# First expert's rows: gathered and transposed in one product, with x as the weights

## The chip, the core and the metric

The kernel runs on one core of a Trainium2 chip. The metric is the device time of one execution in microseconds. Inside the core, TensorE (PE in the profile) multiplies, VectorE (DVE), ScalarE (ACT) and GpSimd (POOL) work on vectors, and SyncE (SP) issues nearly all the DMA transfers. Each of them runs its own list of instructions in order and waits on semaphores for the others.

## The reference

A decoder block on 256 tokens of width 1024, in f32: three groups of attention heads, a memory attention, and then a layer of routed experts. Only the last is touched here:

```
logits = h @ w_router + b_router                  # h = rmsnorm(x), 256 x 1024
gate   = softmax over the 4 largest of 32 logits  # each token picks 4 of 32 experts
for each expert e:
    hh  = h @ w_e1[e] + b_e1[e]                   # 1024 -> 2048, even columns glu, odd columns lin
    act = min(glu, 7) * sigmoid(1.702 glu) * (clip(lin) + 1) * gate
    y  += act @ w_e2[e] + gate * b_e2[e]          # 1024 -> 1024
```

## The kernel before

The expert layer keeps 256 rows of x times a gain in `H` (128 partitions, two row blocks t of 1024 columns). An expert takes at most 64 of the rows in one step (`SLOTS`). The rows are picked by a product with a one-hot matrix: `hot` is 128x64 for each of the two row blocks, with the reciprocal root of the norm in place of the ones. `gather` (L642) uses `hot[:, t, :]` as the weights (64 columns) and 512 columns of `H` as the moving side; the two column halves h go to partitions 0 to 63 and 64 to 127 of one PSUM bank (`B_GATHER`), each half summed over t. That is 4 products. `xg_leaves` (ACT, L1290) copies the bank to `xg`, `turn_gathered` (PE, L653) turns it in 4 transposes, because `multiply_w1` (L693) needs the model dimension on the partitions, and `xgT_leaves` (ACT, L1297) copies the result to `xgT`.

The weights of the experts stream through a ring of 10 slots of 2 MB (`ring`). An expert uses 6 of them: 4 for `w_e1` (two blocks c each), 2 for `w_e2`. SP refills a slot when PE has given it back: the last product of a slot increments `w1_used` (L710) or `w2_used` (L730), for which `load_group` (L889) waits. The 10 slots are filled once before the expert layer begins; slot 0 is the first to be refilled, after the first two blocks c of expert 0 (`multiply_w1(0, ..., 0)` and `(0, ..., 1)`).

For every expert but the first, `gather` and `turn_gathered` stand between blocks of the expert before (L777, L779, L788, L790, and in `step`, L749), where PE has other work. For expert 0 there is none. There the order on PE is (L771 to L776): `gather(0)`, `keep_busy(2)` (two products of the identity with itself, whose result nobody reads), `turn_gathered(0)`, `turn_gates` (L635: two transposes of the gates, which the scatter's biases need), and then the eight `multiply_w1(0, ...)`. DVE makes the first one-hot matrix at L1768 and signals `hot_made`. POOL makes those of the following experts (L1025), into the same tile `hot`, once `gathered` says that the last one has been read. On ACT the order is `xg_leaves(0)`, `xgT_leaves(0)`, `gates_leave` (L1328 to L1330).

A product of f32 operands appears in the trace as two records, a transpose as one.

Of the kernel before, what the change touches and what calls it, by code (L numbers as in the profile page):

```python
# [14 lines left out]
P = 128  # L15
D = 1024
T = 256
NT = T // P
KC = D // P
# [11 lines left out]
SLOTS = 64  # L31
# [28 lines left out]
B_W1, B_W2, B_SCAT, B_GATHER, B_HID = 0, 2, 3, 5, 6  # L60


def build(nc, x, mem, positions, g_mix, w_in, b_forget, g_qa, g_ka, g_cq, g_ckv, w_uq, w_ukv,
# [4 lines left out]
    def at(name, shape, off, dt=F32):  # L68
        return nc.alloc_sbuf_tensor_at(name, shape, dt, offset=base + off)
# [42 lines left out]
    H = at("h_sb", [P, NT, D], Z + 8192)  # L112
    OT = at("heads_T", [P, KC, T], Z + 8192)
    b1T = at("b1_T", [P, E, 16], Z + 16384)
    hot = at("hot_slot", [P, NT, SLOTS], Z + 18432)
# [44 lines left out]
    PS = nc.alloc_psum_tensor("banks", [P, 8, 512], F32)  # L160
# [3 lines left out]
    def S(name):  # L164

        if name not in sems:
            sems[name] = nc.alloc_semaphore(name)
        return sems[name]

    V, G, A, TE = nc.vector, nc.gpsimd, nc.scalar, nc.tensor  # L170
# [67 lines left out]
    def row_cols(q):  # L238

        a = P * W1_ROWS * (q // W1_ROWS) + q % W1_ROWS  # L240
        return slice(a, a + W1_ROWS * (P - 1) + 1, W1_ROWS)

    def hidden_cols(q, par):

        a = 2 * (P * W2_ROWS * (q // W2_ROWS) + q % W2_ROWS) + par
        return slice(a, a + 2 * W2_ROWS * (P - 1) + 1, 2 * W2_ROWS)
# [24 lines left out]
    def _(pe):  # L271
# [26 lines left out]
        def keep_busy(n):  # L298

            pe.wait_ge(S("turned_out"), turn.n - 3)  # L300
            for _ in range(n):
                TE.matmul(PS[:, turn.n % 4, 0:P], ident[:], ident[:], start=True, stop=True)
# [13 lines left out]
        def rows(t):  # L316
            return lambda c: hT[:, c, t * P:(t + 1) * P]
# [62 lines left out]
        for t in range(NT):  # L380
# [4 lines left out]
            for c in range(KC):  # L385
                if (t, c) == (0, KC // 2):
                    pe.wait_ge(S("w_in_cq_rest_in"), 16)
                ins = TE.matmul(bank[:, 0:Q_RANK], rows(t)(c), win["cq"][:, c, :], start=(c == 0), stop=(c == KC - 1))
# [33 lines left out]
        for h in range(FOX_H):  # L422
# [4 lines left out]
                      stop=True).then_inc(S("mm_done"), 1)  # L427
# [71 lines left out]
        for k in range(8):  # L499
            ins = TE.transpose(bank[:, 64 * k:64 * k + 64], b1s[:, hidden_cols(k // 2, k % 2)], ident[0:64, 0:64])  # L500
# [134 lines left out]
        def turn_gates():  # L635

            pe.wait_ge(S("gates_doubled"), 1)
            for t in range(NT):
                ins = TE.transpose(PS[0:3 * E, B_HID, P * t:P * t + P], gate_twice[:, t, :], ident[:])
            ins.then_inc(S("gates_turned"), 1)  # L640

        def gather(i):  # L642

            pe.wait_ge(S("hot_made"), i + 1)
            if not (isinstance(i, int) and i == 0):
                pe.wait_ge(S("xgT_out"), i)
            for t in range(NT):
                for h in range(2):
                    ins = TE.matmul(PS[SLOTS * h:SLOTS * h + SLOTS, B_GATHER, :], hot[:, t, :],  # L649
                                    H[:, t, 512 * h:512 * h + 512], start=(t == 0), stop=(t == NT - 1))  # L650
            ins.then_inc(S("gathered"), 1)

        def turn_gathered(i):  # L653

            pe.wait_ge(S("xg_out"), i + 1)
            for q in range(KC // 2):
                ins = TE.transpose(PS[:, B_GATHER, P * q:P * q + P], xg[:, row_cols(q)], ident[:])  # L657
            ins.then_inc(S("xg_turned"), 1)
# [90 lines left out]
        def step(g, q):  # L749

            i = GROUP * g + (2 + q)
            w1, w2 = of_group(g, PER_STEP * q), of_group(g, PER_STEP * q + W1_UNITS)
            for c in range(KC):
                multiply_w1(i, w1, c)
                if c == AT_TURN:
                    turn_hot(i - 2)
                if c in AT_SCATTER:
                    scatter(i - 2, AT_SCATTER.index(c))
                if c == AT_GATHER:
                    gather(i + 1)  # L760
                if c == AT_GATHER_TURN:
                    turn_gathered(i + 1)
            for k in range(KC // 2):
                multiply_w2(i - 1, w2, k)
                if k == AT_HIDDEN:
                    turn_hidden(i)

        pe.wait_ge(S("turned_out"), turn.n)
        pe.wait_ge(S("mm_out"), len(left_no))
        pe.wait_ge(S("rows_gained"), NT)  # L770
        gather(0)  # L771
        keep_busy(2)
        turn_gathered(0)
        turn_gates()
        for c in range(KC):
            multiply_w1(0, first(0), c)  # L776
            if c == AT_GATHER:  # L777
                gather(1)
            if c == AT_GATHER_TURN:  # L779
                turn_gathered(1)  # L780
# [279 lines left out]
    def _(act):  # L1060
# [212 lines left out]
        for half in range(2):  # L1273
            act.wait_ge(S("mm_out"), left_no[f"mo1{half}"])
            ins = A.activation(junk_x2[:, 512 * half:512 * half + 512], X[:, 1, 512 * half:512 * half + 512], ACT.Square,
                               accum_out=x2_half[:, half:half + 1])
# [4 lines left out]
        for t in range(NT):  # L1281
            ins = A.activation(rt[:, 4, t, 0:E], rt[:, 0, t, 0:E], ACT.Exp, bias=rt[:, 2, t, 0:1])
        ins.then_inc(S("gates_exped"), 1)

        def gates_leave():

            act.wait_ge(S("gates_turned"), 1)
            A.copy(rt_gateT[0:3 * E, :], PS[0:3 * E, B_HID, 0:T]).then_inc(S("gateT_out"), 1)

        def xg_leaves(i):  # L1290

            act.wait_ge(S("gathered"), i + 1)
            if not (isinstance(i, int) and i == 0):
                act.wait_ge(S("xg_turned"), i)
            A.copy(xg[:], PS[:, B_GATHER, :]).then_inc(S("xg_out"), 1)  # L1295

        def xgT_leaves(i):  # L1297

            act.wait_ge(S("xg_turned"), i + 1)
            if not (isinstance(i, int) and i == 0):  # L1300
                act.wait_ge(S("w1_used"), W1_UNITS * i)
            A.copy(xgT[:].rearrange("p q h s -> p (q h s)"), PS[:, B_GATHER, :]).then_inc(S("xgT_out"), 1)
# [22 lines left out]
            act.wait_ge(S("hot_turned"), i + 1)  # L1325
            A.copy(hotT[:], PS[:, B_SCAT, 0:T]).then_inc(S("hotT_out"), 1)  # L1326

        xg_leaves(0)  # L1328
        xgT_leaves(0)
        gates_leave()  # L1330
        xg_leaves(1)
        hidden_leaves(0)
# [549 lines left out]
```

## Time and profile before

| | |
|---|---|
| median of 3 runs | 1132.28 us (1130.17 to 1132.37) |
| the profiled execution, its own time | 1132.49 us |
| its span, first to last instruction | 1130.8 us |
| mean granted TensorE clock | 0.998 |
| PE busy | 1085.5 us (96%), 5069 instructions |
| DVE, ACT, POOL busy | 318.2, 192.1, 138.9 us |
| read from HBM | 427.67 MB, 379 GB/s over the span |

The profiled execution took 0.21 us more than the median of the runs, and 1.7 us of its time lie outside the span. PE's busy time is a modelled one, since its products are pipelined; two products that lie side by side in the array count for themselves.

### The profile page before, as it was taken

How to read it: one execution, taken by the hardware profiler on the slowest of the kernel's cores; microseconds unless marked ns; L12 is line 12 of the kernel's file. 1: busy time of each engine (PE TensorE's matmuls, PEld its weight loads, DVE VectorE, ACT ScalarE, POOL GpSimd, SP SyncE). 2: the span in 40 equal slices, each digit the busy share in tenths (PEclk: the TensorE clock that was granted, in tenths of full speed). 3: DMA queues.
4: the chain of work that ended last, by engine and by line, in shares of the span. 5: the costliest groups of instructions: out<-in, count | busy, mean ns of one | idle time of the engine just before them, and what ended most of it. 6: DMA issues, size and time to landing. Idle time of an engine off the chain costs nothing.

```text
span 1130.8 us, 13638 instructions
## 1 busy us (share of the span) xinstructions
PE 1085.5 (96%) x5069; PEld 439.3 (39%) x5069; DVE 318.2 (28%) x664; ACT 192.1 (17%) x389; POOL 138.9 (12%) x291
## 2 busy tenths in 40 slices
PE   6999999999999999999999999999999999999997
PEld 4566856533333333333333333333333333333332
DVE  4477754412222222222222222222121111222222
ACT  1144433211111111111111111111101111110111
POOL 1032300211111111111111111011111111111100
PEclk9999999999999999999999999999999999999999
DMA  6913376499999999999999999999999999999995
GB/s 225 365 38 150 126 296 281 183 431 426 428 428 427 427 428 429 429 428 428 428 430 429 428 428 429 429 428 429 427 429 429 428 428 428 429 429 428 428 428 235
DMA packets 44024, 429.06 MB, mean 379 GB/s; under 512 B 6336, under 2 KB 13792, under 8 KB 19168
## 3 DMA queue, kind: packets, MB, share of 16 engines
q1 hardware_dynamic: 43376, 427.67, 90.3%
q10 hardware_dynamic: 624, 1.07, 0.2%
q8 instruction: 15, 0.25, 0.1%
q14 instruction: 9, 0.07, 0.0%
HBM read 427.67 MB, written 1.05 MB: 379 GB/s over the span
## 4 chain that ended last, share of the span: by engine, by line
PE 64%; DMA 29%; DVE 3%; SPq 1%; ACT 1%; issue 1%; DVEq 0%
DMA ring<-in_w_e_dram 27%; PE banks L706 27%; PE banks L726 13%; PE banks L313 8%; PE banks L649 4%; PE banks L676 4%; PE banks L739 2%; PE banks L657 2%; DMA w_in_qk<-in_w_in_dram 1%; SPq L830 1%; PE banks L295 1%; PE banks L528 1%; PE banks L330 1%; PE banks L665 1%; PE banks L346 0%
## 5 line engine op out<-in xcount | busy, mean ns | idle before, releaser
L706 PE MATMUL banks<-ring,xg_T 128*64 128x512 f32 x2048 | 478.3, 599 | 24.6 <-DMA ring<-in_w_e_dram 23.5
L706 PEld LDWEIGHTS banks<-ring,xg_T 128*64 128x64 f32 x2048 | 135.8, 136 | 306.3 <-issue 254.3
L726 PE MATMUL banks<-ring,act_T 128*64 128x512 f32 x1024 | 232.9, 596 | 0.4 <-DVE act_T L1828 0.4
L1800 DVE TENSOR_TENSOR x_sb<-x_sb,banks 128x1024 f32<-128x1024 f32 x64 | 78.2, 1221 | 414.9 <-PE banks L676 382.8
L726 PEld LDWEIGHTS banks<-ring,act_T 128*64 128x64 f32 x1024 | 70.3, 137 | 132.5 <-issue 128.1
L1810 DVE TENSOR_TENSOR glu<-banks,b_T 128x512 f32<-128x512 f32 x32 | 22.1, 692 | 242.1 <-PE banks L739 242.1
L1039 POOL COPY picked<-slot_table 128x2 f32 (+1 forms) x32 | 6.0, 188 | 563.2 <-PE banks L665 563.2
L676 PE MATMUL banks<-y_sb,hot_gate_T 64*128 64x512 f32 x256 | 72.0, 640 | 0.8 <-ACT y_sb L1322 0.8
L1309 ACT COPY hidden<-banks 128x1024 f32<-128x1024 f32 x32 | 32.4, 1012 | 206.6 <-PE banks L706 206.6
L1295 ACT COPY xg_rows<-banks 128x512 f32<-128x512 f32 x33 | 19.3, 585 | 271.7 <-PE banks L649 271.7
L649 PE MATMUL banks<-h_sb,hot_slot 128*64 128x512 f32 x264 | 63.0, 598 | 0.9 <-DVE hot_slot L1768 0.9
L1322 ACT COPY y_sb<-banks 128x512 f32<-128x512 f32 x32 | 18.7, 585 | 202.0 <-PE banks L726 202.0
L1043 POOL TENSOR_SCALAR hot_gate<-iota,picked 128x128 f32<-128x128 f32 x64 | 50.1, 791 | 5.5 <-issue 5.5
L739 PEld LDWEIGHTS banks<-ident,hidden 128*128 128x128 f32 x256 | 31.0, 194 | 26.0 <-issue 26.0
L676 PEld LDWEIGHTS banks<-y_sb,hot_gate_T 64*128 64x128 f32 x256 | 19.4, 184 | 52.3 <-issue 51.5
L1828 DVE TENSOR_TENSOR act_T<-lin,sig 128x512 f32<-128x512 f32 x32 | 22.2, 693 | 60.3 <-ACT sig L1316 59.4
L739 PE MATMUL banks<-ident,hidden 128*128 128x128 f32 x256 | 37.1, 288 | 0.0
L1031 POOL TENSOR_SCALAR hot_slot<-iota,picked,stat 128x64 f32<-128x64 f32 x64 | 36.2, 577 | 5.5 <-issue 5.5
L1028 POOL COPY picked<-slot_table 128x2 f32 (+1 forms) x32 | 6.0, 186 | 230.7 <-PE banks L649 230.7
L649 PEld LDWEIGHTS banks<-h_sb,hot_slot 128*64 128x64 f32 x264 | 19.1, 137 | 37.9 <-issue 37.9
L1326 ACT COPY hot_gate_T<-banks 128x256 f32<-128x256 f32 x32 | 11.9, 372 | 100.7 <-PE banks L665 100.7
L313 PE MATMUL banks<-w_out_sb,heads_T 128*128 128x512 f32 x64 | 29.0, 598 | 0.0
(304 smaller groups left out, 774.0 us busy)
## 6 DMA issues: line engine op xcount, KB each, us to landing
ring<-in_w_e_dram SPq DMA_DIRECT2D x190, 2048.0 KB, 37.9
w_out_sb<-in_w_out_dram SPq DMA_DIRECT2D x1, 4096.0 KB, 13.8
ring<-in_w_e_dram SPq DMA_DIRECT2D x4, 1024.0 KB, 40.8
w_in_qk<-in_w_in_dram SPq DMA_DIRECT2D x1, 2048.0 KB, 15.1
w_mkv_sb<-in_w_mkv_dram SPq DMA_DIRECT2D x1, 2048.0 KB, 10.7
w_in_cq<-in_w_in_dram SPq DMA_DIRECT2D x2, 768.0 KB, 8.2
w_in_qc<-in_w_in_dram SPq DMA_DIRECT2D x1, 1536.0 KB, 17.0
w_in_kc<-in_w_in_dram SPq DMA_DIRECT2D x1, 1536.0 KB, 15.1
```

The costliest lines, as they stand in the source:

```text
L313: ins = TE.matmul(bank[:, 0:r.shape[-1]], l, r, start=(c == 0), stop=(c == n - 1))
L649: ins = TE.matmul(PS[SLOTS * h:SLOTS * h + SLOTS, B_GATHER, :], hot[:, t, :], H[:, t, 512 * h:512 * h + 512], start=(t == 0), stop=(t == N ...
L657: ins = TE.transpose(PS[:, B_GATHER, P * q:P * q + P], xg[:, row_cols(q)], ident[:])
L676: ins = TE.matmul(PS[:, first + h, :], hotT[a:a + SLOTS, t * P:(t + 1) * P], Ys[a:a + SLOTS, :], start=True, stop=True)
L706: ins = TE.matmul(PS[SLOTS * h:SLOTS * h + SLOTS, B_W1 + b, :], left, ring[slot][:, 2 * F * j + F * h + 512 * b:2 * F * j + F * h + 512 * ...
L726: ins = TE.matmul(PS[SLOTS * h:SLOTS * h + SLOTS, B_W2, :], actT[:, c % 4, c // 4, :], ring[slot][:, D * j + 512 * h:D * j + 512 * h + 512 ...
L739: ins = TE.transpose(PS[:, B_HID + par, P * q:P * q + P], Hs[:, hidden_cols(q, par)], ident[:])
L1031: ins = G.tensor_scalar(hot[:, t, :], iota[:, 0:SLOTS], pick[:, 0, t:t + 1], y2[t], ALU.is_equal, ALU.mult)
L1043: ins = G.tensor_scalar(hotg[:, t, :], iota[:], pick[:, 1, t:t + 1], pick[:, 2, t:t + 1], ALU.is_equal, ALU.mult)
L1309: A.copy(Hs[:], PS[:, B_W1:B_W1 + 2, :].rearrange("p b n -> p (b n)")).then_inc(S("hidden_out"), 1)
L1800: V.tensor_tensor(X[:, t, :], X[:, t, :], PS[:, first:first + 2, :].rearrange("p b n -> p (b n)"), ALU.add).then_inc(S("added"), 1)
L1828: V.tensor_tensor(actT[:], lin[:], sig[:], ALU.mult).then_inc(S("act_ready"), 1)
```

## The change

For expert 0 alone, gather and transposition become one product with the sides swapped: 128 columns of `H` (every second one, the order that `multiply_w1` wants) are the weights, and `hot[:, t, :]`, 64 columns wide, is the moving side. The result is the transposed rows, and it stands in `B_GATHER` as the four transposes would have left it. `gather(0)`, `keep_busy(2)`, `turn_gathered(0)` and the first `xg_leaves` go. The count `gathered`, for which POOL and ACT wait, is now raised by the first of the two gate transposes, and `xg_out` by a bare semaphore increment on ACT.

```
         def turn_gates():
             pe.wait_ge(S("gates_doubled"), 1)
             for t in range(NT):
                 ins = TE.transpose(PS[0:3 * E, B_HID, P * t:P * t + P], gate_twice[:, t, :], ident[:])
-            ins.then_inc(S("gates_turned"), 1)
+                ins.then_inc(S("gathered" if t == 0 else "gates_turned"), 1)

+        def gather_turned():
+            pe.wait_ge(S("hot_made"), 1)
+            for q in range(KC // 2):
+                for h in range(2):
+                    cols = row_cols(q)
+                    cols = slice(512 * h + cols.start, 512 * h + cols.stop, cols.step)
+                    for t in range(NT):
+                        ins = TE.matmul(PS[:, B_GATHER, P * q + SLOTS * h:P * q + SLOTS * h + SLOTS], H[:, t, cols],
+                                        hot[:, t, :], start=(t == 0), stop=(t == NT - 1))
+            ins.then_inc(S("xg_turned"), 1)

         pe.wait_ge(S("rows_gained"), NT)
-        gather(0)
-        keep_busy(2)
-        turn_gathered(0)
+        gather_turned()
         turn_gates()
         for c in range(KC):
             multiply_w1(0, first(0), c)

-        xg_leaves(0)
         xgT_leaves(0)
+        act.sem_inc(S("xg_out"), 1)
         gates_leave()
```

## Rows read from the trace of the kernel before

**Rows 1.** Page, part 2: 40 slices of the span, PE and DMA busy.
```profile
PE   6999999999999999999999999999999999999997
...
DMA  6913376499999999999999999999999999999995
```
**Rows 2.** Stretches: length, PE busy (records), granted clock, DMA share, GB/s.
```profile
222.50:223.00 0.50, 0.50 (x4) 1.00 0.00 0
...
223.00:223.50 0.50, 0.50 (x4) 1.00 1.07 229
...
230.00:690.00 460.00, 459.41 (x2122) 1.00 1.01 428
...
690.00:1090.00 400.00, 376.71 (x1720) 1.00 1.01 429
...
1114.00:1131.00 17.00, 10.97 (x48) 0.95 0.27 106
```
**Rows 3.** SP's issues of ring slots: start us, us, engine line, transfer, count.
```profile
222.45 3.76 SPq L844 DMA_DIRECT2D ring<-in_w_e_dram  x2
...
231.03 0.33 SPq L844 DMA_DIRECT2D ring<-in_w_e_dram  x1
...
235.30 0.33 SPq L844 DMA_DIRECT2D ring<-in_w_e_dram  x1
...
240.59 5.01 SPq L847 DMA_DIRECT2D ring<-in_w_e_dram  x2
```
**Rows 4.** Timeline, the path from the one-hot matrix to expert 0.
```profile
212.70 0.54 DVE L1768 TENSOR_SCALAR hot_slot<-iota,slot_table,stat 128x64 f32<-128x64 f32 x2
...
213.39 2.60 PE L649 MATMUL banks<-h_sb,hot_slot 128*64 128x512 f32 x8 [0.88 <-DVE hot_slot L1768]
...
215.92 1.22 PE L302 MATMUL banks<-ident 128*128 128x128 f32 x4
...
216.03 0.58 ACT L1295 COPY xg_rows<-banks 128x512 f32<-128x512 f32 x1 [2.15 <-PE banks L649]
...
216.94 1.06 PE L657 MATMUL banks<-ident,xg_rows 128*128 128x128 f32 x4
...
217.79 0.46 PE L639 MATMUL banks<-ident,gate_twice 128*96 128x128 f32 x2
...
218.03 0.58 ACT L1302 COPY xg_T<-banks 128x512 f32<-128x512 f32 x1 [1.42 <-PE banks L657]
...
218.76 8.81 PE L706 MATMUL banks<-ring,xg_T 128*64 128x512 f32 x40 [0.52 <-ACT xg_T L1302]
```
**Rows 5.** Stretches of 0.5 us around it, as in Rows 2.
```profile
212.50:213.00 0.50, 0.01 (x1) 1.00 0.99 426
...
214.00:214.50 0.50, 0.50 (x6) 1.00 0.84 360
...
214.50:215.00 0.50, 0.50 (x4) 0.52 1.07 459
...
217.00:217.50 0.50, 0.50 (x4) 0.50 0.00 0
...
217.50:218.00 0.50, 0.50 (x5) 0.57 0.00 0
```
**Rows 6.** Timeline, gather and transposes of later experts, at full clock.
```profile
246.78 1.89 PE L649 MATMUL banks<-h_sb,hot_slot 128*64 128x512 f32 x8
...
248.72 0.58 ACT L1295 COPY xg_rows<-banks 128x512 f32<-128x512 f32 x1 [4.74 <-PE banks L649]
...
252.03 0.74 PE L657 MATMUL banks<-ident,xg_rows 128*128 128x128 f32 x4
```
**Rows 7.** Timeline, keep_busy's products at full clock.
```profile
209.00 1.28 PE L302 MATMUL banks<-ident 128*128 128x128 f32 x10
```
**Rows 8.** Timeline, products with 128 weight columns and few moving columns; PEld loads weights.
```profile
211.87 0.30 PEld L632 LDWEIGHTS banks<-route,upper 128*128 128x128 f32 x2
...
164.82 1.31 PEld L358 LDWEIGHTS banks<-upper,head_squares 128*128 128x128 f32 x11 [0.24 <-issue]
```
**Rows 9.** Timeline, what stands by the path: DVE's gates, POOL's next matrix, its reader.
```profile
215.00 0.18 DVE L1781 COPY gate_twice<-route 128x64 f32<-128x64 f32 x1
...
216.16 0.18 POOL L1028 COPY picked<-slot_table 128x2 f32<-128x2 f32 x1 [8.28 <-PE banks L649]
...
216.55 1.15 POOL L1031 TENSOR_SCALAR hot_slot<-iota,picked,stat 128x64 f32<-128x64 f32 x2 [0.20 <-issue]
...
227.37 1.92 PE L649 MATMUL banks<-h_sb,hot_slot 128*64 128x512 f32 x8
```

## The prediction

> **What bounds the kernel now.** I read the page's slices first. PE and the DMA engines both show nines from slice 8 on [rows 1]; before that the DMA engines are often idle. Two full rows don't say which of the two sets the end, so the table of stretches comes next: from 230 to 690 us PE is busy for 459.41 of 460 us and the DMA share is 1.01; from 690 to 1090 us PE has 376.71 of 400 us, and the DMA share is still 1.01 [rows 2]. PE is the faster of the two: it lives off the filled ring at first and is starved from 690 us on. The DMA stream is never interrupted. A slot of 2.097 MB at 428 GB/s takes 4.9 us; the 192 slots of the 32 experts less the 10 filled ahead leave 182, and 182 x 4.9 = 892 us. From the moment at which the stream starts, 223.1 us [rows 2], that reaches 1115 us, and from there on the DMA share is low [rows 2]. So the end of the kernel is the start of the stream plus a fixed length plus a fixed tail of PE work. What a change before the expert loop is worth is how much earlier or later SP issues the first refill, at 222.45 us [rows 3].
>
> That refill waits for PE to finish the first two blocks of expert 0. These begin at 218.76 us, when ACT has copied xg_T; in front of this stands a chain in which every engine waits for the one before: the one-hot matrix ready at 213.24, gather 213.39, copy 216.03, transposes 216.94, copy 218.03, expert 0 at 218.76 [rows 4]. It is 5.37 us from 213.39 to 218.76, with nothing beside it. The change rewrites just this chain.
>
> The last thing to read there is the clock. It is full up to 214.5 us, then half (0.50, 1.2 GHz) and full again from about 217.8 us; before the fall PE had little to do (0.01 us of work between 212.5 and 213.0) [rows 5]. The old chain ran mostly at half rate: the gather's 8 records took 2.60 us and the 4 transposes 1.06 us, against 1.89 and 0.74 us at full rate [rows 4, 6].
>
> **Part by part: what goes.** At the full clock the old chain would take 1.89 + 0.05 to the copy [rows 6], 0.58 for the copy, about 0.14 to the transposes, 0.74 + 0.05, 0.58 for the second copy and 0.15 to the first product (218.03 + 0.58 to 218.76 [rows 4]): 4.2 us. All this but the last 0.78 us goes: 3.4 us at full rate, 4.6 us as profiled (213.39 to 218.03). keep_busy's four records (1.22 us [rows 4]) lie beside the first copy, so their removal saves at most the 0.1 us by which they may delay the transposes.
>
> **What comes.** 4 q x 2 h x 2 t = 16 products, 32 records, each with a load of 128 weight columns and a stream of 64 columns. No row shows this shape. The stream alone would be short: 128 columns cost (1.28 - 0.28) / 9 = 0.11 us a record [rows 7], so 64 cost 0.055. The loads decide: with one moving column, 11 loads take 1.31 us, (1.31 - 0.19) / 10 = 0.11 us apart, and with 32 moving columns two are 0.11 apart too (0.30 - 0.19) [rows 8]. The bounds are 0.055 and 0.11 us a record; I take 0.11, since the rows with fewer moving columns than 64 all stand there. The stride of two columns in the weights is new for a load of this kind; the transposes, whose data have that stride too, take 1.06 us for 4 at half rate [rows 4] and 0.74 at full rate [rows 6] and give no sign of more than 0.11 a load. At full rate: 31 x 0.11 + 0.27 for the last = 3.7 us. At half rate a record takes (1.22 - 0.58) / 3 = 0.21 us (keep_busy's, between 215.92 and 217.14 [rows 4]).
>
> The Trainium skill (TensorEngine Tiling (Array Packing), section When to Use Tiling) speaks against this change: where the right-hand side is 64 columns or fewer it advises to swap the sides and to use two column tiles, which is the old form. The same skill (TensorE: Matmul & The Clock Gate, section LDWEIGHTS) has a load last as long as its columns divided by 1.2, 107 ns here, whatever streams; by it the new product is 32 x 0.107 = 3.4 us, an estimate from that page, and [rows 8] agree.
>
> **The sum.** PE's idle time before 213.39 us is untouched, so the clock's fall at 214.5 stays. Until then 1.1 us run at full rate: 10 records. Half rate to 217.8: 3.3 / 0.21 = 15 records. The last 7 at full rate: 0.8 us. The product ends at 213.39 + 1.1 + 3.3 + 0.8 + 0.2 (the last one's tail) = 218.8 us. Then 0.04 + 0.58 for ACT's copy and 0.15: expert 0 begins at 219.5 to 219.6, where it was 218.76. That is 0.8 us later. Never slowed, it would be 213.39 + 3.7 + 0.8 = 217.9, against 213.39 + 4.2 = 217.6 for the old chain, 0.3 us later. The new form trades one copy and its two hand-overs for twice as many weight loads as the old chain had, 32 against 12, each twice as wide as the gather's.
>
> Costed at nothing: turn_gates, 0.46 us [rows 4], now runs beside ACT's copy of 0.58 us, and the gates are ready at 215.18 [rows 9]. POOL's next one-hot matrix waits for `gathered`, now raised behind the whole product, at about 219 instead of 216.1; it needs 0.18 + 0.2 + 1.15 us [rows 9] and is read at 227.37, so 6 us of cover remain; behind it on POOL stand only the following matrices. On ACT the increment costs no copy, and xg_leaves(1) waits for the second gather anyway. The refills behind the first: the stream needs the second at 228, third at 232.9, fourth at 237.8 us, and SP issued them at 225.9, 231.03 and 235.30 [rows 3]; with 0.6 us from issue to the first packet there are 1.2 us and more of slack, and they move together with the first. So a delay at the start goes to the end once, neither more nor less: profiled 1132.49 + 0.8 = 1133.3 us, and against the median 1132.28 + 0.8 = 1133.1 us.
>
> **The rivals** follow.
>
> **Half rate lasts longer (slower).** The new product keeps the array's columns streaming for only half of each record's time, then PE stands for 0.7 us before expert 0 and nothing like keep_busy fills that gap. If the clock does not return at 217.8 us, the product ends 1.1 us later for its last 7 records and tail, and the 16 records before the first refill, 0.215 us each at full rate (1.89 / 8 less the tail [rows 6]), take up to 0.43: together 0.8 + 0.8 = 1.6 us if the clock returns as expert 0 begins, 5 us if only after the first refill. I take the middle, 3.3 us: 1135.6 us. It decides against me if the clock stays at 0.50 beyond about 220 us. For it speaks the half-empty array; against it, that the clock came back in the old chain in spite of its gaps.
>
> **The half rate does not come (faster).** If PE keeps its clock in this chain, expert 0 begins at 217.9, 0.9 us before the profiled one: 1131.4 us. The fall came 1.1 us into the gather, and the runs of before lie 2.2 us apart, about what such a stretch costs, so it may not come every time.
>
> **The stream sets the product (faster).** If loads hide behind one another, 32 x 0.055 = 1.8 us at full rate, about 2.4 with the half-rate part: expert 0 at 216.6, 2.1 us gained: 1130.2 us. [rows 8] speak against it.
>
> **The change does nothing:** were the start of the stream not on the path, the time would stay at 1132.3. [rows 2] speak against it, but a time can't tell it from my forecast.
>
> **How the numbers follow.** Forecast, 0.3 to 1.6 us later: 0.57. Longer half rate: 0.19. No half rate: 0.14. Stream-set: 0.05. Nothing: 0.05. 0.2% is 2.26 us, about what a measurement of this kernel can tell from no change: below 1130.0 or above 1134.5 us. Faster by that takes the stream-set case and a bit of luck: 0.06. Slower takes most of the longer half rate and little else: 0.18. The same: 0.76. The range goes from the stream-set case, 1130.2, to a little beyond the middle of the longer half rate, 1136.2.
>
> **What would show it.** In the profile after: 32 records of the new line, 0.11 us apart at full rate and 0.21 at half, between 213.4 and about 218.8 us; ACT's copy right behind; gate transposes inside that copy; the first record of expert 0 at 219.5 (right if 218.9 to 220.3); half rate over before 218 us; the first refill at 223.2 in place of 222.45, and all later refills and the end later by the same. I am wrong if records stand 0.06 us apart, if the clock stays at 0.50 beyond 220 us, or if the end moves by something other than the first refill.

## The result

| | kernel before | changed kernel |
|---|---|---|
| median | 1131.74 us (10 runs, 1130.17 to 1135.08) | 1135.94 us (10 runs, 1134.05 to 1138.33) |
| ratio | 1 | 1.0029 (95% interval 1.0018 to 1.004) |
| profiled execution, time and span | 1132.49, 1130.8 us | 1134.16, 1132.4 us |
| granted clock of the executions (mean over each) | 0.998 in the profiled one | 0.994 to 0.996 |

The changed kernel is slower by 0.3%. In a second comparison it was 1138.06 us (5 runs) against 1132.29 (29 runs), ratio 1.0045 (1.0032 to 1.0058); the two intervals overlap. The profiled execution of the changed kernel is one of its mildest (1134.16 us of 1134.05 to 1138.33), so the profile shows less than the whole loss.

The page's slices are as before but for PE's first digit and a dip of the clock in the eighth slice, 198 to 226 us (PE, its clock, DMA):

```profile
PE   7999999999999999999999999999999999999997
...
PEclk9999999899999999999999999999999999999999
...
DMA  6913376499999999999999999999999999999995
```

The chain of the changed kernel, from its timeline (start us, us, engine line, records), answers to [rows 4]:

```profile
213.16 5.34 PE L661 MATMUL banks<-hot_slot,h_sb 128*128 128x64 f32 x32 [0.88 <-DVE hot_slot L1778]
...
218.29 0.63 PE L639 MATMUL banks<-ident,gate_twice 128*96 128x128 f32 x2
218.54 0.58 ACT L1312 COPY xg_T<-banks 128x512 f32<-128x512 f32 x1 [4.88 <-PE banks L661]
...
219.27 10.20 PE L718 MATMUL banks<-ring,xg_T 128*64 128x512 f32 x40 [0.34 <-ACT xg_T L1312]
```

From the start of the new product to the first product of expert 0 it takes 6.11 us; the old chain took 5.37 us. The copy follows at once and the gate transposes lie beside it. But that is 0.74 us of a difference that grows: SP issues the first refill at 224.34 us, 11.18 us after the chain began, where it was 9.06 (222.45 less 213.39 [rows 3, 4]). The refills behind it follow as before:

```profile
224.34 0.33 SPq L854 DMA_DIRECT2D ring<-in_w_e_dram  x1
227.78 0.33 SPq L854 DMA_DIRECT2D ring<-in_w_e_dram  x1
232.93 0.33 SPq L854 DMA_DIRECT2D ring<-in_w_e_dram  x1
237.20 0.33 SPq L854 DMA_DIRECT2D ring<-in_w_e_dram  x1
```

The table of stretches (length, PE busy and records, granted clock, DMA share, GB/s) says where the other 1.38 us (11.18 less 9.06 less 0.74) come from:

```profile
215.00:215.50 0.50, 0.50 (x5) 0.79 0.99 426
215.50:222.00 6.50, 6.16 (x25) 0.50 0.09 37
222.00:222.50 0.50, 0.50 (x6) 0.89 0.00 0
...
230.00:690.00 460.00, 459.41 (x2122) 1.00 1.01 428
690.00:1090.00 400.00, 376.94 (x1720) 1.00 1.01 428
```

Half rate begins at about 215.3 us, 2.1 us into the new product, and lasts until about 222.1 us, 2.8 us into the products of expert 0. Before the change it lasted from 214.5 to about 217.9 us [rows 5]: 6.8 us against 3.4. The last two lines match [rows 2] within 0.3 us of PE's busy time: nothing happens to the expert loop itself.

### The profile page after: what moved, and what is told of

Read it like the earlier page. It is cut to its first block, busy times and chain, and to the rows that moved or that the text cites. A ratio compares the mean times of both kernels' runs of the same rounds, so it can differ in the third digit from the quotient of the medians.

```text
span 1132.4 us, 13670 instructions
## 1 busy us (share of the span) xinstructions
PE 1087.5 (96%) x5085; PEld 441.6 (39%) x5085; DVE 317.8 (28%) x664; ACT 191.5 (17%) x388; POOL 139.0 (12%) x291
## 4 chain that ended last, share of the span: by engine, by line
PE 64%; DMA 29%; DVE 3%; SPq 1%; ACT 1%; issue 1%; DVEq 0%
PE banks L718 27%; DMA ring<-in_w_e_dram 27%; PE banks L738 13%; PE banks L313 8%; PE banks L688 4%; PE banks L649 4%; PE banks L751 2%; PE banks L669 1%; DMA w_in_qk<-in_w_in_dram 1%; PE banks L295 1%; SPq L840 1%; PE banks L528 1%; PE banks L330 1%; PE banks L677 1%; PE banks L661 0%
## 5 line engine op out<-in xcount | busy, mean ns | idle before, releaser
L649 PE MATMUL banks<-h_sb,hot_slot 128*64 128x512 f32 x256 | 60.4, 592 | 0.0
```

## The experiments

All kernels were timed in turns with the kernel before. Each timed execution comes with its mean granted clock. I call an execution full-clock when that is 0.999 or 1.000. Of 104 executions of the kernel before, 21 were full-clock, with a median of 1130.88 us; the other 83 have 1132.80 us. So one and the same kernel moves by about 2 us with the clock that it gets. Long losses aren't new either: 28 of the 104 have a mean clock of 0.996 or less.

**The changed kernel again.**

> The changed kernel once more, beside the others. Clock theory (the new product leaves TensorE at half rate longer than the old chain did, 6.8 us instead of 3.4 us in the profiled runs, and that moves the first refill and the end): 3 to 4 us over the kernel before, a half-rate stretch of 6 us or more ahead of the first refill, first refill near 224.3 us. Chain theory (only the longer product counts, the clock is the same with and without the change): 0.7 us over the kernel before.

Measured: 1138.06 us, mean clocks 0.992 to 0.996; none of the 15 executions of the changed kernel in both comparisons was full-clock; all 15 have 0.996 or less, as only 28 of the 104 of the kernel before have. The profile repeats the first one, product of 5.34 us and half rate behind it:

```profile
212.49 5.34 PE L661 MATMUL banks<-hot_slot,h_sb 128*128 128x64 f32 x32 [0.88 <-DVE hot_slot L1778]
218.59 9.77 PE L718 MATMUL banks<-ring,xg_T 128*64 128x512 f32 x38 [0.34 <-ACT xg_T L1312]
...
223.67 0.33 SPq L854 DMA_DIRECT2D ring<-in_w_e_dram  x1
```

5.8 us over the kernel before is more than the clock theory's 3 to 4 and far more than the chain theory's 0.7. Five executions leave the size uncertain, but not the sign or the clock.

**Twice the moving columns under the same loads.**

```
-  TE.matmul(PS[:, B_GATHER, SLOTS * k:SLOTS * (k + 1)], H[:, t, cols], hot[:, t, :], ...)
+  n = 2 if k < 7 else 1                      # k = 2 * q + h
+  TE.matmul(PS[:, B_GATHER, SLOTS * k:SLOTS * (k + n)], H[:, t, cols],
+            hot[:, t, :].unsqueeze(1).to_broadcast([P, n, SLOTS]), ...)
```

> The changed kernel with the moving side of the new product twice as wide: the one-hot columns twice over, 128 instead of 64, the second copy overwritten by the next product. The same 32 weight loads, so the product lasts as long at either rate (0.11 or 0.21 us a record), but columns stream all the time. If the half-empty stream is what keeps the clock down: half rate ends one step sooner (about 218 us, as before the change), first refill near 223.2 us, end 0.8 us over the kernel before. If it is the gap behind the product, or nothing to do with the stream: as the changed kernel, 3 to 4 us over.

Measured: 1133.18 us (11 runs), ratio 1.0009 (0.9998 to 1.0019), against 1.0029 and 1.0045 for the changed kernel. The median is 0.9 us over the kernel before, where 0.8 was expected. Only two executions were full-clock, and the profiled one is one of them: its clock did not come back sooner, it never fell, so it can't show the expected earlier return:

```profile
212.93 3.95 PE L663 MATMUL banks<-hot_slot,h_sb 128*128 128x128 f32 x32 [0.88 <-DVE hot_slot L1781]
...
217.65 8.80 PE L721 MATMUL banks<-ring,xg_T 128*64 128x512 f32 x40 [0.55 <-ACT xg_T L1315]
...
221.33 0.33 SPq L857 DMA_DIRECT2D ring<-in_w_e_dram  x1
```

Adding work to the product makes the kernel faster. At full rate 28 records with 128 columns and 4 with 64 take 3.95 us, as long as 32 with 64 (3.96, next experiment): the second 64 columns are free. That fits a pace set by the loads, which fill 3.85 of the 3.96 us there. The second 64 columns bring back most of the loss, about 2 us by the first ratio and 4 by the second.

**Filler ahead of the product.**

```
-        keep_busy(5)
+        keep_busy(7)          # in front of the ranks
         ...                   # ranks, count
+        keep_busy(4)          # behind the count
```

> The changed kernel with six more keep_busy products ahead of the new product, where TensorE stands idle: two more behind the router (in front of the ranks) and four behind the count. Clock theory: if they keep the clock from falling, the product takes 3.7 us, expert 0 begins at 217.9, first refill at about 221.6 us, the end 0.9 us below the kernel before; the clock shows 1.00 through the chain. Chain theory: no change against the changed kernel. If the fall is only put off, half rate lies in another place and the end is between the two.

Measured: 1133.19 us (11 runs), ratio 1.0002 (0.9992 to 1.0012). Five of 11 executions were full-clock, median 1131.02. In the profiled one, which isn't among the five, the chain has its full clock, and the only half rate before the tail lies elsewhere, behind a wait of 3.17 us for w_in_qk near 30 us (timeline, then stretches):

```profile
31.50 2.93 PE L313 MATMUL banks<-w_in_qk,h_T 128*128 128x512 f32 x3 [3.17 <-DMA w_in_qk<-in_w_in_dram]
...
216.20 3.85 PEld L662 LDWEIGHTS banks<-hot_slot,h_sb 128*128 128x128 f32 x32
216.23 3.96 PE L662 MATMUL banks<-hot_slot,h_sb 128*128 128x64 f32 x32
...
220.96 7.52 PE L719 MATMUL banks<-ring,xg_T 128*64 128x512 f32 x34 [0.55 <-ACT xg_T L1313]
```
```profile
31.00:37.00 6.00, 5.50 (x7) 0.50 1.06 378
...
216.00:220.00 4.00, 4.00 (x35) 1.00 0.80 342
220.00:230.00 10.00, 9.45 (x47) 1.00 0.47 159
```

The chain theory fails: with the very same product the loss is gone. The expected gain of 0.9 us did not come in the median; six of the 11 executions still had a mean clock of 0.998 or less, one of them by the stretch near 30 us.

**The same filler in the kernel before**, once with each group of kernels.

> The kernel before with the same six keep_busy products. Clock theory: chain of 4.2 us instead of 5.4, expert 0 at about 217.6, first refill at 221.3 us, end 1.2 us below the kernel before, and 0.3 us below the changed kernel with the same six. If the product's own length, not the clock, is what the change costs, the difference between these two is the whole 3.3 us that the change cost.

> The kernel before with six keep_busy products ahead of the gather once more, as the neighbour of the next two. Clock theory: at full clock 1130.6 us; within 0.1% of the kernel before in the median.

Measured: 1132.49 us, ratio 1.0000 (0.999 to 1.0009), and 1132.11 us, ratio 0.9996 (0.9986 to 1.0006); 11 of 24 executions were full-clock, median 1130.69. The filler makes such executions more frequent (21 of 104 without it), and the gain of 1.2 us that was expected of the median did not come. Between the two kernels with filler, changed and before, lie 0.7 us by the medians of one and the same comparison (1133.19 and 1132.49), not the 3.3 us expected if the product's own length were the cause. Both profiled executions kept the clock through the chain; the first:

```profile
212.78 1.94 PE L650 MATMUL banks<-h_sb,hot_slot 128*64 128x512 f32 x8
...
216.91 8.80 PE L707 MATMUL banks<-ring,xg_T 128*64 128x512 f32 x40 [0.55 <-ACT xg_T L1303]
...
220.60 0.33 SPq L845 DMA_DIRECT2D ring<-in_w_e_dram  x1
```

The old chain takes 4.13 us at full rate, the new one 4.73 (216.23 to 220.96 above). That is the price of the change without the clock: 0.6 us. The full-clock executions of the two say 0.4 (1131.02 against 1130.63, the median of the six in the same comparison).

**Filler in the gap behind the product.**

```
         gather_turned()
         turn_gates()
+        keep_busy(2)
```

> The changed kernel with keep_busy(2) put back, behind the gate transposes, in the gap in which TensorE waits for ACT's copy. Stream theory (the new product streams columns for only half of each record, and that keeps the clock down): as the changed kernel, the half-rate stretch is already 6.8 us long, at most 0.4 us more where the four records at half rate outlast the copy; 3.5 us or more over the kernel before. Gap theory (the missing filler keeps the clock down): half rate ends one step sooner, 1 us over the kernel before.

Measured: 1135.89 us (12 runs), ratio 1.0023 (1.0013 to 1.0032), no execution full-clock: as the changed kernel, though 2.9 us over the kernel before where 3.5 or more was expected. The profiled execution is the slowest of the twelve (1138.59 us). About 2.6 us of that lie ahead of the chain, and 3.4 us of half rate near 30 us are part of them; the chain shows how far the loss can go: half rate starts within half a microsecond of the product's start and ends behind 226 us, 10.2 us later.

```profile
215.76 6.79 PE L661 MATMUL banks<-hot_slot,h_sb 128*128 128x64 f32 x32 [0.88 <-DVE hot_slot L1779]
...
223.76 10.06 PE L718 MATMUL banks<-ring,xg_T 128*64 128x512 f32 x40
```
```profile
216.00:217.00 1.00, 1.00 (x7) 0.55 0.95 410
217.00:226.00 9.00, 9.00 (x39) 0.50 0.19 79
```

So the missing filler in the gap is not what the changed kernel loses its time by. And since the clock fell 0.3 us into the product here, 2.1 us into it in the two profiles of the changed kernel, the fall is hardly set by the product; it is the return that doesn't come.

**The kernel before without its filler.**

```
         gather(0)
-        keep_busy(2)
         turn_gathered(0)
```

> The kernel before without keep_busy(2) between gather and transposes. If the filler is what brings the clock back after one stretch of 3.4 us, its removal alone lengthens the stretch: 1.5 us or more over the kernel before, clock 0.997 and less in most runs. If the old products, whose columns stream all the time, do it: no change, within 0.3 us.

Measured: 1133.76 us against 1133.03, ratio 1.0003 (0.999 to 1.0015), 3 of 12 executions full-clock. The time tells no difference, but it doesn't exclude the 1.5 us either, since the interval reaches 1.7 us. The one profiled execution has a long stretch of half rate, 6.8 us, which ends 1.9 us into expert 0:

```profile
215.00:221.00 6.00, 4.98 (x16) 0.50 0.22 94
```

So a long stretch isn't reserved to the new product, and what that filler contributes in the old chain stays open.

**Wide stream and filler ahead together.**

> The changed kernel with the moving side twice as wide and with the six keep_busy products ahead of it. Clock theory: no half rate in the chain at all, so the new product stands against the old chain at full clock: runs whose clock is 1.00 lie 0.3 us above such runs of the kernel before with the same filler (1130.6 us), at 1130.9 us; other runs are slower only where another stretch of half rate, as the one at 30 us, has come in. Chain theory: 0.7 us or more over.

Measured: 1131.89 us (12 runs) against 1133.03, ratio 0.999 (0.9979 to 1.0); 9 of 12 executions were full-clock, median 1131.29, which is 0.4 us over the full-clock executions of the kernel before and 0.6 over those with the filler (1130.69). With the clock held, the change costs what its chain is longer.

**The product twice.**

```
+        gather_turned(inc=False)     # the same 16 products, no semaphore
         gather_turned()
```

> The changed kernel with the new product issued twice, one behind the other (64 records instead of 32, same result). Load theory: 32 more records at 0.11 us (full clock) to 0.21 us (half rate): the chain is 3.5 to 6.8 us longer, and since the clock stays at half rate through them, nearer to 6.8; expert 0 begins at about 225.5 us, the end 6 us over the changed kernel, 9 to 10 us over the kernel before. If something hides behind a record (stream-set): 1.8 to 3.5 us over the changed kernel.

Measured: 1143.31 us (5 runs), ratio 1.0096 (1.0077 to 1.0114). That is 10.3 us over the kernel before and 7.4 over the changed kernel, which was timed in another comparison (1135.94 us).

```profile
213.05 12.64 PE L661 MATMUL banks<-hot_slot,h_sb 128*128 128x64 f32 x64 [0.88 <-DVE hot_slot L1780]
...
226.46 10.09 PE L719 MATMUL banks<-ring,xg_T 128*64 128x512 f32 x34 [0.34 <-ACT xg_T L1314]
...
232.71 0.33 SPq L856 DMA_DIRECT2D ring<-in_w_e_dram  x1
```
```profile
215.00:231.00 16.00, 15.66 (x65) 0.50 0.06 26
231.00:232.00 1.00, 1.00 (x4) 0.67 0.00 0
```

The second copy adds 7.3 us (12.64 less 5.34), a little over 32 x 0.21 = 6.8, because less of the first copy is at full rate here. Half rate goes on for as long as the product does, and 5 us into expert 0: 11 us of products without a pause do not bring the clock back. Twice the product costs two to three times as much (1.0096 against 1.0045 and 1.0029), and the stream-set rival (at most 3.5 us more) falls.

**A plain delay at full clock.**

```
         turn_gates()
+        keep_busy(18)                # on top of the filler ahead, in the kernel before
```

> The same with keep_busy(18) behind the gate transposes: 36 records of 0.11 us, 4.0 us, of which 0.7 lie beside ACT's copy. They are dense and keep the clock, so this is a plain delay of expert 0 by 3.3 us. If the end follows the first refill one to one: 3.3 us over its neighbour. If the ring hides it, since TensorE runs ahead of the DMA stream later: 0. If half a microsecond of slack lies between: 2.8.

Measured: 1134.70 us (11 runs) against 1132.41, ratio 1.0026 (1.0017 to 1.0036). The six full-clock executions have 1134.13 us against 1130.92 of the neighbour: 3.2 us. The profiled chain grew from 4.13 to 7.54 us, 3.4 us:

```profile
213.21 1.94 PE L650 MATMUL banks<-h_sb,hot_slot 128*64 128x512 f32 x8
...
216.63 4.18 PE L302 MATMUL banks<-ident 128*128 128x128 f32 x36
...
220.75 8.80 PE L707 MATMUL banks<-ring,xg_T 128*64 128x512 f32 x40
```

The end follows the first refill one to one. The same can be read without an experiment, from every profile: span less the issue of the first refill.

| profiled execution of | chain, us | first refill, us | span, us | difference |
|---|---|---|---|---|
| kernel before | 5.37 | 222.45 | 1130.8 | 908.4 |
| changed kernel | 6.11 | 224.34 | 1132.4 | 908.1 |
| wide stream | 4.72 | 221.33 | 1129.4 | 908.1 |
| filler ahead, changed | 4.73 | 224.64 | 1132.5 | 907.9 |
| filler ahead, before | 4.13 | 220.60 | 1128.6 | 908.0 |
| filler in the gap | 8.00 | 228.72 | 1136.7 | 908.0 |
| product twice | 13.41 | 232.71 | 1140.9 | 908.2 |
| plain delay | 7.54 | 224.44 | 1132.5 | 908.1 |

Over 12 us of difference in the first refill the rest of the kernel stays within 0.5 us. The six profiles that the table leaves out lie inside the same bounds (907.9 to 908.3).

**A version that gains.** The filler ahead does nothing for the stretch near 30 us, so filler went there too, into the wait for w_in_qk:

```
         for t in range(NT):
             project("ckv", t)
+        keep_busy(8)                 # or keep_busy(4)
         for t in range(NT):
             project("qk", t)
```

> The kernel with the six fillers ahead of the gather, and eight keep_busy products more in the wait for w_in_qk near 30 us, where the changed kernel with fillers lost its clock in its profiled execution. Clock theory: slow clock runs (0.998 and less) become rare, median 1130.9 us, 1.3 us below the kernel before. Against it: where the transfer is not late the eight products stand in front of the projections for 1.2 us (1.8 us less the 0.6 us of wait), and the median gains nothing.

> As the kernel with fillers ahead of the gather and eight in the wait near 30 us, but with four products there (0.9 us) instead of eight (1.8 us). Clock theory: if four are enough to keep the clock, nearly all runs show 0.999 or 1.00 and the median is 1131.2 us, 1.2 us below the kernel before; if they are too few, slow clock runs return and the median is that of the fillers ahead alone, 1132.2 us.

Measured: with eight, 1131.50 us against 1132.41, ratio 0.9994 (0.9985 to 1.0003), all 11 executions full-clock; with four, 1131.29 against 1132.48, ratio 0.9989 (0.9978 to 0.9999), 11 of 12 full-clock. Both hold the clock. Eight stand in the way where the wait is short, as expected: their full-clock executions have 1131.50 us, 0.6 more than those of the kernel before. The kernel with four is the one with the lowest ratio, 1.2 us below the kernel before by the medians, as expected. Its interval only just leaves out no change, and it is the best of eleven kernels tried, so the gain is likely but not proven.

## Why the prediction was right or wrong

The median, 1135.94 us, lies in the range given, 1130.2 to 1136.2, near its upper end. The likeliest case was not the one that came: the forecast of 1133.1 us and 0.76 for no difference missed a loss clear of noise, and the rival "half rate lasts longer" (1135.6 us, chance 0.19) is what happened.

The range held in part by luck. The second comparison's median, 1138.06 us, lies outside it. The rival's price was a middle taken between 1.6 and 5 us, and it has a slip: the text finds 1.1 us for the last seven records and the tail, but adds 0.8; with 1.1 the ends are 1.9 and 5.3 us.

- What bounds the kernel: right. The DMA stream sets the time from the first refill to the end, one to one, as the plain delay and the table above show.
- The bound of a record, 0.11 us at full rate: right in kind, a little small. At full rate 32 records took 3.96 us, about (3.96 - 0.28) / 31 = 0.12 us each, where the sum had 3.7 us for all. The 3.4 us that the prediction sets beside it is further off: the loads follow one another at 0.12 us, but each lasts 0.20 us at full rate (median 196 ns) and 0.33 at half (331 ns in the product issued twice). The stream-set case (0.055) falls by the same row. The price at full clock was put at 0.3 us and is 0.6 (4.73 against 4.13): the product's extra 0.26 us is nearly all of it.
- The half-rate record, 0.21 us: right. It took 6.79 us for 32 records that ran almost wholly at half rate (filler in the gap).
- The length of the product and the start of expert 0: right by luck. The product took 5.34 us where the sum had 5.4, and expert 0 began 6.11 us into the chain against a predicted 6.1 to 6.2. But the sum had 1.1 us at full rate, 3.3 at half and the rest at full again; measured were 2.1 us at full rate and all the rest at half. The later fall and the missing return cancelled.
- "The clock's fall at 214.5 stays" and "Half rate to 217.8": wrong, and the second is the step that failed. It took the end of the half-rate stretch from the trace of before as if it were fixed in time, though the work in that stretch is just what the change replaces. In the new chain half rate went on to 222.1 us, into expert 0, whose first two blocks took from 219.27 to the refill at 224.34, 5.07 us instead of 3.69. The rival priced just this, at 1.6 to 5 us. The profiled executions show +2.1 us to the refill, and the one with filler in the gap +3.9 (12.96 less 9.06).
- Why it went on: it hangs on the stream. Same loads, same duration, twice the columns, and most of the loss is gone. In all four profiles in which the clock fell at the 64-column product it never came back while the product ran, for 3.2, 3.2, 6.4 and 11.1 us at half rate, but only 2.6 to 5.2 us after expert 0 had begun. That the 128-column product would bring it back sooner is argued from its median; the one profile of that kernel has no fall. The stream isn't the only thing that counts, since the kernel before without its filler shows a stretch of 6.8 us too. The rival named two suspects, the half-empty stream and the gap without filler; the second, taken alone, is cleared by the filler in the gap. That a better filled TensorE ahead of the product removes the loss too (ratio 1.0002) fits: there the clock need not come back if it doesn't fall.
- The Trainium skill's advice (TensorEngine Tiling (Array Packing), When to Use Tiling) to make a 64-column operand the weights, in two column tiles, is borne out: the old chain is 0.6 us shorter at full clock, and the kernel with it 0.3 to 0.45% faster, most of which is the clock's part. The two column tiles do run side by side in the trace: at full clock the records of the gather at 246.78 us [rows 6] start in pairs, 0.007 us apart, and a pair takes 0.43 us.
- Costed at nothing: the gate transposes beside the copy, POOL's later one-hot matrix, ACT's increment. Right; the second gather waits for none of them, and refills two to four follow the first as before (3.44, 5.15 and 4.27 us apart, before 8.58 for the first two steps together and 4.27 [rows 3]).
- The spread of the runs of before was laid to the clock as a guess. The 104 executions bear this out: 1130.88 us where the clock was full, 1132.80 where it wasn't.

Left open: whether the loss is nearer to 0.29 or to 0.45%; where executions without a profile lose their clock (only the mean is known for them, and part of it may be lost near 30 us rather than in the chain); what decides whether the clock falls at all; and the part of keep_busy(2) in the old chain.

## What to carry to other kernels

Count weight loads, not only columns: where a product streams fewer columns than its weights have, the loads can set the time (0.12 us a record for 128 weight columns here, with 64 columns streaming as with 128), and merging two small products into one can cost more than the copy that it saves. A granted clock read from the old trace belongs to the old work: if the change replaces the work inside or behind a half-rate stretch, price the stretch's end as unknown, and add what stands behind it at half rate. And where one stream binds from a certain moment to the end, measure every change ahead of it by that moment; span less that moment was constant here (907.9 to 908.4 us), and any profile can confirm it.

## What was not expected of the hardware

Streaming 128 columns instead of 64 under loads of 128 weight columns cost no time at all (3.95 against 3.96 us for 32 records). And far from the changed place three of the 14 profiled executions fell to 0.50 of the clock, for 3.4 to 6.8 us, in or right after a wait for w_in_qk near 30 us. Those waits were 3.17, 3.15 and 2.25 us long, but five other executions waited 2.46 to 3.04 us there and kept their clock, so the length of the wait does not decide it. Four spare products of the identity there, with the six ahead of the gather, left 11 of 12 executions with full clock, against 11 of 24 with the six alone and 21 of 104 with none.
